# First feed-forward product in two sums: both parts of the input behind one load of the high weights

## The chip, the core and the metric

The kernel runs on one core of a Trainium2 chip. The metric is the device time of one execution in microseconds (us), the median of several runs. Weights and inputs lie in HBM as float32; the kernel loads them, computes on the core's engines (TensorE, VectorE, ScalarE, GpSimd, and SyncE for the transfers) and writes a result of 256 x 1024.

## The reference

A first block of other layers is followed by two layers like this one (`DEPTH_2` is 2, the width 1024, 256 tokens, the inner width 4096):

```python
for l in range(DEPTH_2):
    h = _rms_norm(x, attn_norm[l])
    ...
    x = x + mixed @ w_out[l]
    h = _rms_norm(x, mlp_norm[l])
    x = x + jnp.square(jax.nn.relu(h @ w_ff1[l])) @ w_ff2[l]
return _rms_norm(x, final_norm)
```

The change touches `h @ w_ff1[l]` and what stands right around it: the relu and the square behind it, and the start of `... @ w_ff2[l]`.

## The kernel before

**Split numbers.** Products of the layers are made of float32 values in two parts of the type float32r: `high`, the rounded value, and `low`, the rest. A product is then high x high, plus high weights x low input, plus low weights x high input. The input of the first feed-forward product lies in `xh` and `xl`, each 128 partitions x (8 chunks of 256 tokens), viewed as `xhT` and `xlT`.

**Units.** Weights come in units of 512 KB (128 x 1024), through a ring of four slots (class `Ring`). For each unit ScalarE makes the high part (`Ring.round`, L184, the rounding) and GpSimd the low part (`Ring.subtract`, L199). Both parts have two buffers, so the rounding of unit n waits until TensorE is done with all of unit n - 2, and the subtraction of unit n for its rounding. Every engine runs its instructions in the order of its own program; waits are on semaphores.

**The stage.** The first feed-forward product has 32 units, 128 of the 4096 inner columns each. Two units make a pair i (0 to 15), one PSUM bank of 512 float32: unit 2i fills its columns 0 to 255, unit 2i + 1 the rest. `split_pair` (L1998 on) issues 24 matmuls per unit, all at L2008: 8 with high weights and `xhT`, 8 with high weights and `xlT`, 8 with low weights and `xhT`, 256 columns each.

What follows for each pair i:
- `relu(i)` on VectorE (L1966), in the bank, over 512 columns
- `hidden(i)` on ScalarE: Square in the bank (L1701), then a Copy into `hidden_hi` (L1703)
- `hidden_low(i)` on VectorE (L1972): bank minus `hidden_hi` into `hidden_lo`; with it the bank is released

VectorE issues `relu(i)` and then `hidden_low(i - 1)`. ScalarE's loop (i from 1 to 15) issues a rounding, then `hidden(i - 1)` (pairs 0 and 1 at i = 3, pairs 2 and 3 at i = 4), then a second rounding. The first waits for the end of unit 2i, the second for the end of unit 2i + 1.

**Banks.** Class `Banks` hands the eight banks of PSUM to named jobs by a plan made ahead (L1490 to L1496). `open` on TensorE waits until all earlier jobs of that bank were given back (`give`); `take` on another engine waits until the bank is full. Before, pairs 0 and 1 hold banks 4 and 5, pairs 2 to 5 the banks 0 to 3, and pairs 6 to 15 the banks 4 to 6 in turn. Bank 7 holds constants.

**The second product** follows: 32 units of 24 matmuls (L2306), which sum into banks 0 to 3. All four are opened ahead of its first matmul:

```python
out_banks = [banks.open(pe, ("f2", l, b)) for b in range(4)]
for u in range(FF2_UNITS):
    high = ring.high(pe)
    banks.wait_drained(pe, ("f", l, u // 2))
```

Other places that the text refers to: the down rows of the mixture stage ahead of the layers (`down_row`, L2627 and L2634), 12 matmuls of 512 columns per row of weights, of the same types; the square roots and row sums of the layers (L1994, L1559); the attention's transposes (L422 to L424) and the output product of the attention (`branch`, L2064, L2069).

Of the kernel before, what the change touches and what calls it, by code (L numbers as in the profile page):

```python
# [20 lines left out]
F32R = mybir.dt.float32r  # L21
# [249 lines left out]
def build(nc, stop_after, xT, consts, par1, bias1, w1, keys, wu, wv, par2, w2, out):  # L271
    ctx = ExitStack()
    with ctx:
        def sb(name, cols, dt=F32):
            return ctx.enter_context(nc.sbuf_tensor(name, [P, cols], dt))

        def sem(name):
            return ctx.enter_context(nc.semaphore(name))
# [7 lines left out]

        xh, xl = sb("xh", DC * T, F32R), sb("xl", DC * T, F32R)
        wh, wl = sb("wh", 2 * SLOT, F32R), sb("wl", 2 * SLOT, F32R)
# [5 lines left out]
        arena = memory.enter_context(nc.sbuf_tensor("arena", [P, ARENA], F32))  # L294
        xhT, xlT = (x[:, :].rearrange("p (c t) -> p c t", t=T) for x in (xh, xl))
        whv, wlv = (x[:, :].rearrange("p (b n) -> p b n", b=2) for x in (wh, wl))
# [31 lines left out]
        def two(ap, w=T):  # L328
            return ap.rearrange("p (a b) -> p a b", b=w)
# [62 lines left out]
        def pairs_of(names):  # L392

            return [x for n in names for x in (None, n)]
# [993 lines left out]
        def lview(at, a, b):  # L1388
            return lpart(at, at + a * b).rearrange("p (a b) -> p a b", b=b)
# [53 lines left out]
        MLA, SELECTED, WINDOW = 2, 0, 1  # L1443
        l_pre, l_tiles = sem("squares_added"), sem("tile_sum_matrix")
        tile_sum = small[:, 1792:1824]
        nsa_heads = [[2 * c, 2 * c + 1, 8 + 2 * c, 9 + 2 * c] for c in range(4)]
# [9 lines left out]
        for l in range(LAYERS):  # L1456
# [34 lines left out]
            banks.turn = 0  # L1491
            banks.plan([("f", l, i) for i in range(2, 6)], low4)
            banks.turn = 0
            banks.plan([("f", l, i) for i in range(6, 16)], mid3)
            for b in low4:
# [6 lines left out]
            ring.plan(banks, [("wn", l, i) for i in range(4)] + [("wm", l, i) for i in range(4)]  # L1502
                      + pairs_of([("f", l, i) for i in range(16)]) + [None] * 31 + [("f2", l, 3)], True)
        banks.plan([("end", 0)], (4,))
# [34 lines left out]
        def layers_act(act):  # L1539
# [34 lines left out]
            for l in range(LAYERS):  # L1574
# [122 lines left out]
                def hidden(i):  # L1697
# [5 lines left out]
                    act.activation(hidden_hi[:, 2 * i:2 * i + 2, :], two(b[:, :]), ACT.Copy).then_inc(l_fhi, 1)  # L1703

                for i in range(1, 16):
                    ring.round(act, 1)
                    if i == 3:
                        hidden(0)
                        hidden(1)
                    elif i == 4:  # L1710
                        hidden(2)
                        hidden(3)
                    elif i > 4:
                        hidden(i - 1)
                    ring.round(act, 1)
                hidden(15)
                ring.round(act, FF2_UNITS - 2)
# [7 lines left out]
        def layers_dve(dve):  # L1725
# [29 lines left out]
            for l in range(LAYERS):  # L1755
# [212 lines left out]
                def hidden_low(i):  # L1968
# [4 lines left out]
                                                 ALU.subtract), ("f", l, i))  # L1973

                for i in range(17):
                    if i < 16:
                        relu(i)
                    if i:
                        hidden_low(i - 1)
# [7 lines left out]
        def layers_pe(pe):  # L1987
# [91 lines left out]
            for l in range(LAYERS):  # L2079
# [212 lines left out]
                for i in range(4):  # L2292
                    branch(("wm", l, i), l, 4, i == 0)
                    if i == 0:
                        sums(("mm", l), (1,), added, ready=(l_pre, 6 * l + 4))
                for i in range(16):
                    split_pair(("f", l, i), 2 * l + 1 if i == 0 else None)
                    if i == 1:
                        sums(("mf", l), range(2), added, ready=(l_pre, 6 * l + 6))
# [564 lines left out]
```

## Time and profile before

| | |
|---|---|
| median of 3 runs | 1742.39 us (1741.98 to 1742.43) |
| the profiled execution | 1742.68 us, of which 1740.9 us from the first to the last instruction (the span) |
| mean granted TensorE clock | 0.990 |
| TensorE (PE) busy | 1651.7 us, 95% |
| VectorE (DVE) busy | 895.1 us, 51% |
| ScalarE (ACT) busy | 917.8 us, 53% |
| GpSimd (POOL) busy | 1193.6 us, 69% |
| HBM read | 277.3 MB, 160 GB/s over the span |

Times in the trace are in us from the start of the span. PE is TensorE's matmuls and PEld its weight loads, which run beside them. A matmul's duration in a row is longer than the distance to the next, since matmuls are pipelined; distances are read from start to start. In brackets stands how long the engine had been idle and what released it. The first feed-forward product runs from about 1201 to 1299 us in the first layer and from about 1539 to 1637 us in the second.

### The profile page before, as it was taken

Reading aid. Unit: us, or ns where it says so; the run is one execution under the profiler, and the core shown is the slowest. Engines: PE = TensorE matmul, PEld = TensorE weight load, DVE = VectorE, ACT = ScalarE, POOL = GpSimd, SP = SyncE. Lnnn points to the kernel's source line nnn. Section 1 sums busy time; section 2 is a strip of 40 time slices with the busy share of each in tenths; the row PEclk is TensorE's granted clock in tenths of the full one; section 3 lists DMA queues with packets and bytes.
Section 4 is the critical chain, followed back from the end, with each engine's and each line's share of the span. In section 5 each row is a group of like instructions: output and inputs, shape, how many; then the busy total and the mean of one; then the engine's idle time right before and its main releaser. Section 6 shows DMA issues by size and latency. Waiting matters only on the chain.

```text
span 1740.9 us, 32150 instructions
## 1 busy us (share of the span) xinstructions
PE 1651.7 (95%) x12786; PEld 1506.7 (87%) x12786; DVE 895.1 (51%) x1888; ACT 917.8 (53%) x1541; POOL 1193.6 (69%) x500
## 2 busy tenths in 40 slices
PE   6988999999999999999999999888999998989997
PEld 6976999999999998777788888667999986789997
DVE  6978446991266665788611115866220067652101
ACT  5576655444543435555566665565553446655532
POOL 4552777888777777777788887115888861168885
PEclk9999999999999999999999999999999999999999
DMA  6432555655555555555566664513656654145663
GB/s 209 159 103 68 184 166 172 182 183 181 174 166 167 163 169 165 164 169 166 182 193 193 193 194 144 178 46 116 179 184 183 187 153 157 50 133 183 185 190 110
DMA packets 79604, 280.43 MB, mean 161 GB/s; under 512 B 8672, under 2 KB 9440, under 8 KB 79200
## 3 DMA queue, kind: packets, MB, share of 16 engines
q1 hardware_dynamic: 79456, 278.38, 51.8%
q8 instruction: 102, 1.67, 0.4%
q14 instruction: 46, 0.38, 0.1%
HBM read 277.30 MB, written 1.05 MB: 160 GB/s over the span
## 4 chain that ended last, share of the span: by engine, by line
PE 63%; issue 4%; DVE 3%; POOL 2%; ACT 1%; POOLq 0%; DVEq 0%; ACTq 0%
PE ps L2627 14%; PE ps L2008 12%; PE ps L2306 10%; PE ps L2634 7%; PE ps L2605 4%; PE ps L2606 3%; PE ps L2610 3%; POOL wl L199 2%; PE ps L2064 1%; PE ps L2591 1%; PE ps L371 1%; PE ps L2593 1%; PE ps L2130 1%; DVE small L390 1%; PE ps L2069 1%
## 5 line engine op out<-in xcount | busy, mean ns | idle before, releaser
L199 POOL TENSOR_TENSOR wl<-slots,wh 128x1024 fp32r<-128x1024 f32 x236 | 569.7, 2417 | 377.9 <-ACT wh L184 370.8
L2413 POOL TENSOR_TENSOR wl<-slots,wh 128x1024 fp32r<-128x1024 f32 x256 | 619.1, 2420 | 153.5 <-ACT wh L2353 151.4
L2353 ACT ACTIVATE wh<-slots 128x1024 fp32r<-128x1024 f32 x256 | 271.3, 1060 | 378.9 <-issue 244.9
L184 ACT ACTIVATE wh<-slots 128x1024 fp32r<-128x1024 f32 x236 | 249.4, 1060 | 263.5 <-PE ps L2306 105.5
L2605 PE MATMUL ps<-xh,wh 128*128 128x256 f32 x1024 | 255.6, 287 | 0.9 <-ACT small L2392 0.9
L2606 PE MATMUL ps<-xl,wh 128*128 128x256 f32 x1024 | 250.4, 282 | 0.0
L2605 PEld LDWEIGHTS ps<-xh,wh 128*128 128x128 f32 x1024 | 195.5, 191 | 1.2 <-ACT small L2392 1.1
L2606 PEld LDWEIGHTS ps<-xl,wh 128*128 128x128 f32 x1024 | 195.9, 191 | 0.0
L2627 PE MATMUL ps<-wh,xh 128*128 128x512 f32 x508 | 162.1, 400 | 2.8 <-DVE xl L2539 2.8
L2627 PE MATMUL ps<-wh,xl 128*128 128x512 f32 x508 | 157.7, 392 | 0.0
L2610 PE MATMUL ps<-xh,wl 128*128 128x256 f32 x1024 | 143.6, 283 | 0.6 <-POOL wl L2413 0.6
L2539 DVE TENSOR_TENSOR xl<-ps,xh 128x256 fp32r<-128x256 f32 x127 | 53.9, 424 | 161.8 <-ACT xh L2369 161.7
L2634 PE MATMUL ps<-wl,xh 128*128 128x512 f32 x508 | 136.3, 390 | 0.0
L2610 PEld LDWEIGHTS ps<-xh,wl 128*128 128x128 f32 x1024 | 132.1, 192 | 0.8 <-POOL wl L2413 0.8
L2306 PE MATMUL ps<-hidden_hi,wh 128*128 128x256 f32 x512 | 124.3, 280 | 1.9 <-POOL wl L199 1.9
L2306 PE MATMUL ps<-hidden_lo,wh 128*128 128x256 f32 x512 | 124.0, 279 | 0.0
L2634 PEld LDWEIGHTS ps<-wl,xh 128*128 128x128 f32 x508 | 95.4, 188 | 20.9
L2627 PEld LDWEIGHTS ps<-wh,xl 128*128 128x128 f32 x508 | 95.3, 188 | 20.6
L2008 PE MATMUL ps<-xh,wh 128*128 128x256 f32 x704 | 105.8, 289 | 6.9 <-ACT wh L184 4.6
L2627 PEld LDWEIGHTS ps<-wh,xh 128*128 128x128 f32 x508 | 91.0, 189 | 19.2 <-issue 3.2
L2008 PEld LDWEIGHTS ps<-xh,wh 128*128 128x128 f32 x704 | 92.4, 191 | 13.4 <-issue 8.0
L2531 DVE SCALAR_TENSOR_TENSOR arena<-ps,arena 128x256 f32<-128x256 f32 x128 | 54.0, 423 | 94.3 <-PE ps L2593 94.3
(383 smaller groups left out, 3140.5 us busy)
## 6 DMA issues: line engine op xcount, KB each, us to landing
slots<-w SPq DMA_DIRECT2D x260, 512.0 KB, 3.6
slots<-wu SPq DMA_DIRECT2D x128, 512.0 KB, 3.5
slots<-wv SPq DMA_DIRECT2D x128, 512.0 KB, 3.5
arena<-bias SPq DMA_DIRECT2D x1, 2048.0 KB, 8.1
h<-xT SPq DMA_DIRECT2D x2, 512.0 KB, 5.4
arena<-keys SPq DMA_DIRECT2D x1, 1024.0 KB, 5.7
yT<-y_out SPq DMA_DIRECT2D x2, 512.0 KB, 2.7
layer<-consts SPq DMA_DIRECT2D x1, 800.0 KB, 5.3
```

The source lines that it names most:

```text
L184: act.activation(self.hi[:, n % 2, :], self.slots[:, u % SLOTS, :], ACT.Copy).then_inc(self.rounded, 1)
L199: pool.tensor_tensor(self.lo[:, n % 2, :], self.slots[:, self.order[n] % SLOTS, :], self.hi[:, n % 2, :].bitcast(F32), ALU.subtract).then_ ...
L2008: ins = pe.matmul(halves[j], w[:, k, :], x[:, k, :], start=(first and k == 0), stop=(last and k == DC - 1), skip_group_check=True)
L2306: return pe.matmul(out_banks[c // 2][:, (c % 2) * T:(c % 2 + 1) * T], w[:, c * P:(c + 1) * P], x[:, u, :], start=start, stop=False, skip_g ...
L2353: act.activation(whv[:, r % 2, :], slots_v[:, r % SLOTS, :], ACT.Copy).then_inc(w_hi, 1)
L2413: pool.tensor_tensor(wlv[:, r % 2, :], slots_v[:, r % SLOTS, :], whv[:, r % 2, :].bitcast(F32), ALU.subtract).then_inc(w_lo, 1)
L2531: dve.scalar_tensor_tensor(a, grid, 1.0 / GATE_SCALE, a, ALU.mult, ALU.mult).then_inc(g_done, 1)
L2605: pe.matmul(out, hi[:, k, :], xhT[:, k, :], start=(k == 0), stop=False)
L2606: ins = pe.matmul(out, hi[:, k, :], xlT[:, k, :], start=False, stop=False)
L2610: ins = pe.matmul(out, lo[:, k, :], xhT[:, k, :], start=False, stop=(k == DC - 1))
L2627: ins = pe.matmul(psum[2 * t + half], part_a[:, tokens], hi[:, half * 512:(half + 1) * 512], start=begins, stop=False, skip_group_check=True)
L2634: ins = pe.matmul(psum[2 * t + half], a_hi[:, t * P:(t + 1) * P], lo[:, half * 512:(half + 1) * 512], start=False, stop=(row == NE2 - 1), ...
```

## The change

Pairs 2 to 15 are computed otherwise; pairs 0 and 1 stay. `xh` and `xl` become two halves of one tensor, so that one view, `x_parts[:, :, k, :]`, gives chunk k of both parts, 2 x 256 columns. A unit now has a bank of its own (jobs `f` and `f_second`). Eight matmuls of 512 columns with the high weights leave two sums in it, one per input part, and eight matmuls of 256 columns with the low weights add to the first. ScalarE copies the second sum into SBUF (`keep_second`), and VectorE adds it to the first (`add_halves`); for the pair's second unit the sum is written into the other half of the bank of `f`, after which `relu`, `hidden` and `hidden_low` go on as before, and the bank of `f_second` is given back. The 28 jobs of a layer take banks 0 to 6 in turn.

```diff
-        xh, xl = sb("xh", DC * T, F32R), sb("xl", DC * T, F32R)
+        both = sb("x_parts", 2 * DC * T, F32R)
+        xh, xl = both[:, 0:DC * T], both[:, DC * T:2 * DC * T]
+        x_parts = both[:, :].rearrange("p (k c t) -> p k c t", k=2, t=T)
...
+        l_half, l_both = sem("second_half_kept"), sem("halves_added")
+        second_half = lview(5888, 2, T)
...
             banks.turn = 0
-            banks.plan([("f", l, i) for i in range(2, 6)], low4)
-            banks.turn = 0
-            banks.plan([("f", l, i) for i in range(6, 16)], mid3)
+            banks.plan([(n, l, i) for i in range(2, 16) for n in ("f", "f_second")], seven)
             for b in low4:
                 banks.plan([("f2", l, b)], (b,))
...
-                      + pairs_of([("f", l, i) for i in range(16)]) + [None] * 31 + [("f2", l, 3)], True)
+                      + pairs_of([("f", l, i) for i in range(2)])
+                      + [(n, l, i) for i in range(2, 16) for n in ("f", "f_second")] + [None] * 31 + [("f2", l, 3)], True)
...
+                def keep_second(i, j):
+
+                    b = banks.take(act, (("f", "f_second")[j], l, i))
+                    if j == 0 and 14 * l + i > 2:
+                        act.wait_ge(l_both, 14 * l + i - 2)
+                    elif j == 1 and i > 2:
+                        banks.wait_drained(act, ("f_second", l, i - 1))
+                    act.activation(second_half[:, j, :], b[:, T:2 * T], ACT.Copy).then_inc(l_half, 1)
+
                 for i in range(1, 16):
                     ring.round(act, 1)
                     if i == 3:
                         hidden(0)
                         hidden(1)
                     elif i == 4:
                         hidden(2)
                         hidden(3)
                     elif i > 4:
                         hidden(i - 1)
+                    if i >= 2:
+                        keep_second(i, 0)
                     ring.round(act, 1)
+                    if i >= 2:
+                        keep_second(i, 1)
                 hidden(15)
...
+                def add_halves(i):
+
+                    b = banks.take(dve, ("f", l, i))
+                    dve.wait_ge(l_half, 28 * l + 2 * (i - 2) + 1)
+                    dve.tensor_tensor(b[:, 0:T], b[:, 0:T], second_half[:, 0, :], ALU.add).then_inc(l_both, 1)
+                    other = banks.take(dve, ("f_second", l, i))
+                    dve.wait_ge(l_half, 28 * l + 2 * (i - 2) + 2)
+                    banks.give(dve.tensor_tensor(b[:, T:2 * T], other[:, 0:T], second_half[:, 1, :], ALU.add),
+                               ("f_second", l, i))
+                    dve.wait_ge(l_both, 14 * l + i - 1)
+                    banks.wait_drained(dve, ("f_second", l, i))
+
                 for i in range(17):
+                    if 2 <= i < 16:
+                        add_halves(i)
                     if i < 16:
                         relu(i)
                     if i:
                         hidden_low(i - 1)
...
+                def wide_unit(job):
+
+                    bank = banks.open(pe, job)
+                    w = ring.high(pe).rearrange("p (k n) -> p k n", k=DC)
+                    for k in range(DC):
+                        pe.matmul(two(bank[:, :]), w[:, k, :], x_parts[:, :, k, :], start=(k == 0), stop=False,
+                                  skip_group_check=True)
+                    w = ring.low(pe).rearrange("p (k n) -> p k n", k=DC)
+                    for k in range(DC):
+                        ins = pe.matmul(bank[:, 0:T], w[:, k, :], xhT[:, k, :], start=False, stop=(k == DC - 1),
+                                        skip_group_check=True)
+                    banks.close(ins, job)
+
                 for i in range(16):
+                    if i >= 2:
+                        wide_unit(("f", l, i))
+                        wide_unit(("f_second", l, i))
+                        continue
                     split_pair(("f", l, i), 2 * l + 1 if i == 0 else None)
```

## Rows read from the trace of the kernel before

**Rows 1.** The page, busy time, share of the span and instructions of the engines.

```profile
PE 1651.7 (95%) x12786; PEld 1506.7 (87%) x12786; DVE 895.1 (51%) x1888; ACT 917.8 (53%) x1541; POOL 1193.6 (69%) x500
```

**Rows 2.** Busy time by window, main stretch of the stage in both layers.

```profile
core 0: us, PE busy (x) PEld busy (x) DVE busy (x) ACT busy (x) POOL busy (x), PEclk, DMA share, GB/s
1221.19:1298.95 77.76, 77.76 (x650) 77.76 (x649) 17.26 (x27) 44.69 (x57) 65.32 (x28) 1.00 0.61 185
1559.23:1637.00 77.77, 77.77 (x651) 77.77 (x650) 17.26 (x27) 44.68 (x57) 65.33 (x28) 1.00 0.59 185
```

**Rows 3.** Timeline of TensorE, one unit and the next one's start: start, length, instructions.

```profile
1247.12 1.12 PE L2008 MATMUL ps<-xh,wh 128*128 128x256 f32 x8
1248.08 1.12 PE L2008 MATMUL ps<-xl,wh 128*128 128x256 f32 x8
...
1249.99 1.12 PE L2008 MATMUL ps<-xh,wh 128*128 128x256 f32 x8
```

**Rows 4.** Busy time by window, down rows of the mixture stage (columns as in rows 2).

```profile
868.80:1010.25 141.45, 141.45 (x626) 117.13 (x625) 22.13 (x52) 87.01 (x157) 125.17 (x53) 1.00 0.63 193
```

**Rows 5.** The chain that ended last, near pair 2's first unit: start, length, what.

```profile
1217.69 2.40 POOL wl L199
1220.09 0.04 issue
```

**Rows 6.** Groups of instructions by shape, ScalarE, 256 columns from PSUM (mean ns second).

```profile
L1545 ACT ACTIVATE xh<-ps,layer_par 128x256 fp32r<-128x256 f32 x32 | 12.3, 482 | 4.6 <-DVE ps L1955 1.9 <-DVE ps L1731 1.5 <-DVE ps L1752 1.2
L1630 ACT ACTIVATE attention<-ps 128x256 f32<-128x256 f32 x16 | 6.1, 384 | 16.0 <-PE ps L2130 16.0
```

**Rows 7.** Groups of instructions by shape, VectorE, 256 columns with one input from PSUM.

```profile
L2508 DVE TENSOR_TENSOR ps<-ps,small 128x256 f32<-128x256 f32 x128 | 54.1, 423 | 0.1
L2539 DVE TENSOR_TENSOR xl<-ps,xh 128x256 fp32r<-128x256 f32 x127 | 53.9, 424 | 161.8 <-ACT xh L2369 161.7
```

**Rows 8.** Timeline of ScalarE in the stage, a rounding and pair 0's Square and Copy.

```profile
1227.21 1.06 ACT L184 ACTIVATE wh<-slots 128x1024 fp32r<-128x1024 f32 x1 [1.82 <-PE ps L2008]
1228.18 0.58 ACT L1701 ACTIVATE ps<-ps 128x512 f32<-128x512 f32 x1
1228.79 0.60 ACT L1703 ACTIVATE hidden_hi<-ps 128x512 fp32r<-128x512 f32 x1
1229.29 0.60 ACT L1701 ACTIVATE ps<-ps 128x512 f32<-128x512 f32 x1
```

**Rows 9.** Timeline of VectorE in the stage, `hidden_low(0)` and the relu behind it.

```profile
1229.49 0.69 DVE L1972 TENSOR_TENSOR hidden_lo<-ps,hidden_hi 128x512 fp32r<-128x512 f32 x1 [9.71 <-ACT hidden_hi L1703]
1230.10 0.69 DVE L1966 SCALAR_TENSOR_TENSOR ps<-ps,rst 128x512 f32<-128x512 f32 x1
```

**Rows 10.** Timeline of all engines where the second product starts, first layer.

```profile
1298.95 0.28 PE L2306 MATMUL ps<-hidden_hi,wh 128*128 128x256 f32 x1
...
1299.21 1.06 ACT L184 ACTIVATE wh<-slots 128x1024 fp32r<-128x1024 f32 x1 [0.70 <-PE ps L2008]
```

**Rows 11.** Timeline of TensorE around three gaps of the attention part.

```profile
1112.69 1.96 PE L2194 MATMUL ps<-attention,slots 128*128 128x256 f32 x8 [2.48 <-issue]
...
1139.21 0.45 PE L422 MATMUL ps<-cst,attention 128*128 128x128 f32 x1 [3.06 <-issue]
...
1169.23 0.71 PE L1994 MATMUL ps<-small,cst 128*128 128x256 f32 x2 [2.07 <-DVE small L390]
1169.55 2.10 PE L2064 MATMUL ps<-mix_hi,wh 128*128 128x256 f32 x8
1171.45 1.86 PE L2064 MATMUL ps<-mix_lo,wh 128*128 128x256 f32 x8
1173.16 1.10 PE L2069 MATMUL ps<-mix_hi,wl 128*128 128x256 f32 x8
1174.10 1.10 PE L2064 MATMUL ps<-mix_hi,wh 128*128 128x256 f32 x8
1175.03 1.10 PE L2064 MATMUL ps<-mix_lo,wh 128*128 128x256 f32 x8
```

**Rows 12.** Busy time and granted clock by window, behind or at the same gaps.

```profile
1140.00:1142.00 2.00, 2.00 (x11) 1.88 (x10) 1.90 (x7) 1.47 (x3) 2.00 (x2) 0.50 0.00 0
1170.00:1172.00 2.00, 2.00 (x11) 2.00 (x11) 0.46 (x1) 2.00 (x8) 1.64 (x1) 0.50 0.04 8
1111.00:1114.00 3.00, 1.31 (x6) 1.21 (x7) 1.49 (x2) 1.64 (x7) 0.00 (x0) 1.00 1.02 412
```

More of the change, by code:

```diff
@@ L294, in build @@
         arena = memory.enter_context(nc.sbuf_tensor("arena", [P, ARENA], F32))
-        xhT, xlT = (x[:, :].rearrange("p (c t) -> p c t", t=T) for x in (xh, xl))
+        xhT, xlT = (x.rearrange("p (c t) -> p c t", t=T) for x in (xh, xl))
         whv, wlv = (x[:, :].rearrange("p (b n) -> p b n", b=2) for x in (wh, wl))
```

## The prediction

> **What bounds the kernel now.** I read the page's share of busy time first: TensorE is busy for 95% of the span, every other engine for 69% or less [rows 1]. Then the same numbers by stretch, because the change touches one stage only, the first feed-forward product of the two layers. In both layers its main stretch is 77.76 us long and TensorE is busy for all of it, at full granted clock, with GpSimd at 65 us and ScalarE at 45 us [rows 2]. So TensorE sets the time of the stage, and a shorter unit of TensorE work is worth its full length as long as nothing else becomes late. The stretch holds 27 of the stage's 32 units, 2.880 us each; a group of eight 256-column matmuls takes 0.96 us, that is 120 ns a matmul, 24 to a unit [rows 3].
>
> **What the change removes.** In a changed unit the 16 matmuls with high weights become 8 of 512 columns. The trace has 512-column matmuls of the same types, in the down rows of the mixture stage: 52 rows of 12 in 141.45 us, so 226.7 ns each [rows 4]. A unit becomes 8 x 226.7 + 8 x 120 = 2.773 us, 0.107 us less. Pairs 2 to 15 change, 28 units in a layer. The first of them gains nothing: its low weights wait for GpSimd, whose subtraction ends at 1220.09, and TensorE goes on at 1220.13 [rows 5]; the subtraction's start doesn't depend on the high part. Gain: 27 x 0.107 = 2.88 us a layer, 5.8 us in all. The one difference from the down rows is that the 512 moving columns lie in two pieces of 256, 8 KB apart in a partition. No row shows such a read. The bounds for the wide matmul are 213 ns (512 columns at 2.4 GHz) and 240 ns (no gain over two of 256); I take 226.7, since the engine reads column by column either way.
>
> By the Trainium skill, "TensorE: Matmul & The Clock Gate", section "Back-to-back issue gap", a matmul costs its columns at 2.4 GHz plus 2.5 ns, so that joining two saves only 2.5 ns. Rows 3 and 4 disagree: 256 columns cost 13.3 ns over their 106.7, and 512 cost 13.4 ns over their 213.3.
>
> **What it adds, with cover.** ScalarE gets two copies of 256 columns per pair, the rows nearest being 384 and 482 ns [rows 6]; I take 0.42. VectorE gets two additions of 256 columns, 424 ns each [rows 7], and waits for its own result. With pairs of 5.55 us, ScalarE holds two roundings (0.97 each, start to start), Square and Copy (1.11) and the copies (0.8): 3.9 us [rows 8]. VectorE holds 0.9 + 0.6 + 0.7 = 2.2 us [rows 9]. Both fit. Does order fit? After a unit ends, ScalarE starts the next rounding 0.26 us later [rows 10], GpSimd subtracts for 2.4 us [rows 5], and the result is there about 3.8 us after the unit's end; TensorE asks for it 2.77 + 1.81 = 4.6 us after. The work in front of the second rounding (rounding, Square, Copy, copy: 0.26 + 0.97 + 1.11 + 0.42 = 2.76) ends just as that rounding becomes due at 2.77 + 0.26. The steady state is hidden at no cost; if cover were missing by x, it would cost x on each of 28 pairs once the slack of 0.8 us is used.
>
> **Banks.** The plan now gives seven banks in turn to (f, f_second) of pairs 2 to 15. That moves two waits.
> (a) f of pair 4 gets bank 4, which pair 0 held. Pair 0 is released by `hidden_low(0)`, which waits for ScalarE's Square and Copy, and those stand behind the rounding that waits for f of pair 3. Before, that bank was asked for much later, by pair 6. With units of 2.773 from 1221.19 on, where the window of rows 2 begins, f of pair 3 is the second unit and ends at 1226.74. Rounding starts 0.26 later, the Copy 1.58 after that (0.97 + 0.61) and takes 0.60; 0.10 to VectorE, 0.69 for the subtraction, 0.04 to TensorE: 1230.0 [rows 5, 8, 9, 10]. TensorE wants the bank after the third unit, at 1229.51. Cost 0.5 us a layer. Just behind it ScalarE has two hidden pairs and two copies to do, its rounding comes 0.8 us late, and TensorE waits some 0.1 us more; 0 to 0.6 are the bounds.
> (b) Counting on, pair 14's f is job 24 of the turn, so bank 3; pairs 12 and 13 hold banks 0 to 2 last. The second product opens banks 0 to 3 before its first matmul. Before, pairs 2 to 5 held these banks last, and the second product started with no gap at 1298.95 [rows 10]. Now TensorE waits for `hidden_low(14)`. In VectorE's program that stands behind `add_halves(15)` and `relu(15)`, and `add_halves(15)` needs the very last unit and ScalarE's copy of it, which itself stands behind a rounding that waits for the same unit. From the end of the last unit (time 0): rounding starts 0.26 [rows 10]; the copy at 1.23 [rows 8]; done 1.65; VectorE 0.10 later adds for 0.42, until 2.17; 0.04 for its own wait (taken as TensorE's); `relu(15)` starts at 2.21 and `hidden_low(14)` 0.61 behind it, at 2.82; plus 0.68 is 3.50; plus 0.04 [rows 5 to 9]. TensorE stands for 3.5 us, once a layer. Bounds: 3.3 (copy at 384 ns, no wait between) and 3.8. Nothing gives it back: the second product is TensorE's alone, with GpSimd at 2.4 us of each 2.8 us unit, and rounding for its third unit can't start before its first ends.
>
> **Clock.** Such a gap has a second price. In the attention part TensorE stood for 3.06 us and for 2.07 us, and behind each the granted clock is 0.50, that is 1.2 GHz of 2.4; after a gap of 2.48 us it stayed at 1.00 [rows 11, 12]. The same holds in the other layer, where the gaps repeat. Behind the 2.07 us gap two groups of eight take 1.90 and 1.71 us from start to start where such a group takes 0.93: 1.75 us lost [rows 11]. The new gap of 3.5 us is longer than all of these, so I expect the fall. Bounds 0 and 1.75; I take 1.6, because part of the slow stretch may lie in the gap itself.
>
> **Sum.** Per layer: -2.88 + 0.5 + 0.1 + 3.5 + 1.6 = +2.8 us. Two layers: +5.6. The profiled execution took 1742.68 us (span 1740.9), 0.3 above the median of 1742.39, so the forecast for the median is 1748.0 us.
>
> **The rivals.**
> 1. The hand-over stall is there, but the clock stays up, in one layer or both. For: the 2.48 us gap left it alone. Against: two of three kinds of gap did not, and this one is longer. Without any fall, 2 x 1.2 = +2.4: 1744.8 us. With one, 1746.4.
> 2. Joining saves nothing, because the fixed cost is not per matmul or the two pieces read slower. Then the 5.8 us stay: 1753.8 us. Against: rows 3 and 4 give the same 13 ns for both widths. The skill's rule named above goes most of the way there; by it alone the saving would be 54 x 8 x 2.5 ns = 1.1 us, an estimate from that page, and the time 1752.7.
> 3. ScalarE's longer queue makes the second rounding late in each pair, not only near pair 4. For: its margin before that rounding is only 0.3 us. Against: 0.8 us of slack behind it at TensorE. It decides from about 1.1 us of lateness; at 0.3 us a pair it costs 28 x 0.3 = 8 us: 1756 us. Also against: the copies' nearest rows leave no room for 1.1 us.
> 4. The other side: bank 3 does not bind at the hand-over, as when pair 14 is released ahead of the last unit (a slip in my count of the turn, or in the order of VectorE's program). The stall and the clock's fall go together: -2 x 2.88 + 2 x 0.6 = -4.6, so 1737.8 us. It decides from a stall below 2.3 us a layer without a fall. For: only the release of one bank separates the cases. Against: job 24 of seven is 3, and the code issues `hidden_low(i - 1)` behind `add_halves(i)` and `relu(i)`.
> 5. The bank or copy waits are shorter than I price them, by up to 1 us a layer, and the clock falls in one layer: 2 x (-2.88 + 0.6 + 2.5) + 1.6 = +2.0, 1744.4 us.
>
> **Numbers.** Forecast 0.52; rival 1 0.18, half within 0.2%; rival 2 0.08; rival 3 0.06; rival 4 0.08; rival 5 0.08. A change of 0.2%, 3.5 us, is about what a measurement of this kernel can tell from none: 1738.9 to 1745.9 is "same". Faster 0.08, same 0.09 + 0.08 = 0.17, slower 0.75. The range runs from 1744.3 (rival 5; rival 1 without a fall is just above) to 1754.5 (rival 2, with the bounds of a and b on the forecast); it leaves out rivals 3 and 4.
>
> **What would show it.** In the profile after: a changed unit of 2.77 us, wide matmuls 227 ns apart; a gap on TensorE of about 0.5 us ahead of pair 4; a gap of 3.5 us ahead of each first matmul of the second product, ended by VectorE's `hidden_lo`; a granted clock of 0.50 behind it for some 3 us; the stage itself about 2.2 us shorter a layer, and the second product late by what I say. A wide matmul 240 ns apart, a hand-over without a gap, or a TensorE wait for GpSimd in each pair would prove me wrong, each at its own step.

## The result, and the profile after

The median of five runs is 1751.88 us (1749.43 to 1752.61), beside 1742.43 us for five runs of the kernel before (1741.98 to 1745.21). The ratio is 1.0047, with a 95% interval of 1.0033 to 1.0062: the change makes the kernel slower by 9.5 us where 5.6 were forecast. The profiled execution took 1751.99 us, its span is 1750.2.

The page of after, the answer to rows 1. TensorE has 448 matmuls fewer and is busy for longer:

```profile
PE 1654.2 (95%) x12338; PEld 1489.0 (85%) x12338; DVE 918.7 (52%) x1944; ACT 933.6 (53%) x1597; POOL 1193.2 (68%) x500
```

**Where the time is.** I set the same points of TensorE's program side by side, each by the start of the matmul there.

| point | before | after | behind by | gained since |
|---|---|---|---|---|
| first layer begins | 1051.29 | 1051.30 | 0.0 | |
| pair 2 begins | 1217.75 | 1218.57 | 0.8 | +0.8 |
| second product begins | 1298.95 | 1301.89 | 2.9 | +2.1 |
| second layer begins | 1390.59 | 1395.58 | 5.0 | +2.1 |
| its pair 2 begins | 1555.79 | 1560.35 | 4.6 | -0.4 |
| its second product begins | 1636.99 | 1643.66 | 6.7 | +2.1 |
| last matmul of it | 1728.49 | 1737.81 | 9.3 | +2.6 |

So both products of both layers lose. The 0.8 us ahead of the first pair 2 is outside the change: the granted clock falls once more there, in the attention part. It falls behind the very gap of 2.4 us that left the clock alone in the trace of before [rows 11, 12] (window of after, columns as in rows 2):

```profile
1113.60:1116.60 3.00, 3.00 (x18) 2.26 (x18) 1.65 (x4) 2.98 (x12) 0.00 (x0) 0.50 0.63 258
```

The -0.4 us between the start of the second layer and its pair 2 lies outside the change as well.

The main stretch of the stage in after, to be read against rows 2 (busy time by window, same columns). It is 76.02 us where it was 77.76, and a gap now follows it that the stretch doesn't include:

```profile
1222.01:1298.03 76.02, 75.69 (x434) 66.31 (x432) 28.39 (x53) 52.19 (x84) 64.97 (x28) 1.00 0.59 189
```

The timeline of TensorE in after, against rows 3: a wide group, a low group, and so on. Eight wide matmuls take 1.84 us from start to start and the low ones 0.95, a unit 2.79 us (2.88 before). The third row to the last shows the wait ahead of pair 4:

```profile
1224.81 2.00 PE L2332 MATMUL ps<-x_parts,wh 128*128 128x512 f32 x8
1226.65 1.12 PE L2336 MATMUL ps<-x_parts,wl 128*128 128x256 f32 x8
1227.60 2.00 PE L2332 MATMUL ps<-x_parts,wh 128*128 128x512 f32 x8
1229.44 1.11 PE L2336 MATMUL ps<-x_parts,wl 128*128 128x256 f32 x8
1230.89 2.11 PE L2332 MATMUL ps<-x_parts,wh 128*128 128x512 f32 x8 [0.34 <-DVE hidden_lo L1988]
1232.84 1.11 PE L2336 MATMUL ps<-x_parts,wl 128*128 128x256 f32 x8
1233.79 2.00 PE L2332 MATMUL ps<-x_parts,wh 128*128 128x512 f32 x8
```

The hand-over, as the chain that ended last has it in after (start, length, what). It is the answer to rows 10, where the second product followed without a gap. Read down: the last low group, ScalarE's rounding, its copy of the second sum, VectorE's second addition, `relu(15)`, `hidden_low(14)`, and then the second product. The trace calls `second_half` by the name of the tensor that it lies in, `attention`:

```profile
1297.24 0.96 PE ps L2336 x8
...
1298.28 0.04 ACT wh L184
...
1299.25 0.37 ACT attention L1715
...
1299.71 0.44 DVE ps L1998
...
1300.24 0.06 DVE ps L1982
1300.30 0.55 issue
1300.84 0.69 DVE hidden_lo L1988
1301.54 0.35 issue
1301.89 1.20 PE ps L2354 x4
```

The last 0.35 us, between the end of `hidden_low(14)` and the first matmul, hold three wait instructions of TensorE's own program, about 0.11 us from one to the next. The first is the wait for bank 3 itself, in `open` (L106). Behind it stand that of `ring.high` (L213) and that for pair 0 in the second product's loop (L126), whose work had long been done. `PEldq` is the sequencer of TensorE's weight loads. Each has one row (shortest, median and longest duration in ns, first and last start):

```profile
L106 PEldq EVENT_SEMAPHORE  x1: 51/51/51, 1301.6 to 1301.6; - x1
L213 PEldq EVENT_SEMAPHORE  x1: 51/51/51, 1301.7 to 1301.7; - x1
L126 PEldq EVENT_SEMAPHORE  x1: 51/51/51, 1301.8 to 1301.8; - x1
```

Behind the hand-over the second product starts slowly. The timeline of TensorE in after: matmuls stand 0.21 us apart where they stand 0.12 before and later.

```profile
1301.89 0.55 PE L2354 MATMUL ps<-hidden_hi,wh 128*128 128x256 f32 x1 [3.70 <-DVE hidden_lo L1988]
1302.24 0.42 PE L2354 MATMUL ps<-hidden_lo,wh 128*128 128x256 f32 x1
...
1305.44 1.91 PE L2354 MATMUL ps<-hidden_hi,wl 128*128 128x256 f32 x8
1307.15 0.41 PE L2354 MATMUL ps<-hidden_hi,wh 128*128 128x256 f32 x1
...
1309.43 1.10 PE L2354 MATMUL ps<-hidden_hi,wl 128*128 128x256 f32 x8
```

Busy time and granted clock by window for it, both layers (columns as in rows 2):

```profile
1302.00:1308.00 6.00, 6.00 (x28) 6.00 (x29) 0.69 (x1) 0.73 (x2) 0.00 (x0) 0.50 0.28 88
1644.00:1649.00 5.00, 5.00 (x25) 5.00 (x25) 0.69 (x1) 0.00 (x0) 0.00 (x0) 0.50 0.35 108
```

**The first layer's account.** The stretch: -1.74 us. From the end of the last unit, 1298.03, to the second product, 1301.89: +3.86. The first two units of the second product take 5.26 and 3.21 us where they took 2.83 each: +2.81, the clock. The rest of the second product, from its third unit to the next layer, takes 85.22 us where it took 85.98: -0.76. With the +0.8 from ahead of the stage this is the 5.0 of the table. In the second layer the first two units take 5.26 and 3.04 us, +2.64, and the rest takes as long as before: its units are 2.83 us there, and 2.80 in the first layer. So the 0.76 us came in one layer only.

### The profile page after: what moved, and what is told of

Read it like the earlier page. It is cut to its first block, busy times and chain, and to the rows that moved or that the text cites. A ratio compares the mean times of both kernels' runs of the same rounds, so it can differ in the third digit from the quotient of the medians.

```text
span 1750.2 us, 31531 instructions
## 1 busy us (share of the span) xinstructions
PE 1654.2 (95%) x12338; PEld 1489.0 (85%) x12338; DVE 918.7 (52%) x1944; ACT 933.6 (53%) x1597; POOL 1193.2 (68%) x500
## 4 chain that ended last, share of the span: by engine, by line
PE 64%; issue 3%; DVE 3%; POOL 2%; ACT 1%; POOLq 0%; DVEq 0%; ACTq 0%
PE ps L2675 14%; PE ps L2354 10%; PE ps L2682 7%; PE ps L2332 5%; PE ps L2653 4%; PE ps L2654 3%; PE ps L2658 3%; PE ps L2038 3%; PE ps L2336 3%; POOL wl L199 1%; PE ps L2094 1%; PE ps L2639 1%; PE ps L2106 1%; PE ps L373 1%; PE ps L2641 1%
## 5 line engine op out<-in xcount | busy, mean ns | idle before, releaser
L2675 PE MATMUL ps<-wh,x_parts 128*128 128x512 f32 x1016 | 258.2, 396 | 2.8 <-DVE x_parts L2587 2.8
L2653 PE MATMUL ps<-x_parts,wh 128*128 128x256 f32 x1024 | 255.5, 287 | 0.9 <-ACT small L2440 0.9
L2654 PE MATMUL ps<-x_parts,wh 128*128 128x256 f32 x1024 | 250.4, 282 | 0.0
L2675 PEld LDWEIGHTS ps<-wh,x_parts 128*128 128x128 f32 x1016 | 186.3, 188 | 39.8 <-issue 3.2
L2653 PEld LDWEIGHTS ps<-x_parts,wh 128*128 128x128 f32 x1024 | 195.5, 191 | 1.2 <-ACT small L2440 1.1
L2654 PEld LDWEIGHTS ps<-x_parts,wh 128*128 128x128 f32 x1024 | 195.9, 191 | 0.0
L2658 PE MATMUL ps<-x_parts,wl 128*128 128x256 f32 x1024 | 143.6, 283 | 0.6 <-POOL wl L2461 0.6
L2682 PE MATMUL ps<-wl,x_parts 128*128 128x512 f32 x508 | 136.3, 390 | 0.0
L2658 PEld LDWEIGHTS ps<-x_parts,wl 128*128 128x128 f32 x1024 | 132.1, 192 | 0.8 <-POOL wl L2461 0.8
L538 PE MATMUL ps<-x_parts,wh 128*128 128x256 f32 x736 | 105.2, 298 | 22.7 <-ACT wh L184 9.4
L538 PEld LDWEIGHTS ps<-x_parts,wh 128*128 128x128 f32 x736 | 98.3, 203 | 27.3 <-ACT wh L184 15.8
L2332 PE MATMUL ps<-x_parts,wh 128*128 128x512 f32 x448 | 112.5, 393 | 3.9 <-ACT wh L184 3.2
L2682 PEld LDWEIGHTS ps<-wl,x_parts 128*128 128x128 f32 x508 | 95.4, 188 | 21.0
L2354 PEld LDWEIGHTS ps<-hidden_hi,wh 128*128 128x128 f32 x512 | 98.8, 193 | 10.0 <-issue 10.0
```

The lines of the kernel that those rows point to most:

```text
L538: ins = pe.matmul(halves[j], w[:, k, :], x[:, k, :], start=(first and k == 0), stop=(last and k == DC - 1), skip_group_check=True)
L2332: pe.matmul(two(bank[:, :]), w[:, k, :], x_parts[:, :, k, :], start=(k == 0), stop=False, skip_group_check=True)
L2354: return pe.matmul(out_banks[c // 2][:, (c % 2) * T:(c % 2 + 1) * T], w[:, c * P:(c + 1) * P], x[:, u, :], start=start, stop=False, skip_g ...
L2653: pe.matmul(out, hi[:, k, :], xhT[:, k, :], start=(k == 0), stop=False)
L2654: ins = pe.matmul(out, hi[:, k, :], xlT[:, k, :], start=False, stop=False)
L2658: ins = pe.matmul(out, lo[:, k, :], xhT[:, k, :], start=False, stop=(k == DC - 1))
```

## The experiments

Theory: the wide matmuls gain what their spacing says, and a late release of bank 3 makes the gap, behind which the clock falls. Rivals: the loss sits in something that the additions or copies do in each pair; the slow start isn't the clock's; the gap would be given back. Ratios are to runs of the kernel before that were made beside those of the experiments: 21 runs for `e1_banks` to `e4_best` (1741.7 to 1746.3 us) and 31 for `e5_adjacent` to `e8_order` (1740.9 to 1748.1). A difference of two ratios carries both intervals, some 3 us either way. Each trace shows one execution.

**Only the last four banks** (`e1_banks`). The kernel after with

```diff
-            banks.plan([(n, l, i) for i in range(2, 16) for n in ("f", "f_second")], seven)
+            banks.plan([(n, l, i) for i in range(2, 14) for n in ("f", "f_second")], seven)
+            for n, i, b in (("f", 14, 4), ("f_second", 14, 5), ("f", 15, 6), ("f_second", 15, 5)):
+                banks.plan([(n, l, i)], (b,))
```

> The kernel after, with one edit: the last four jobs (f and f_second of pairs 14 and 15) take banks 4, 5, 6, 5 and not 3, 4, 5, 6, so no bank that the second product opens is held by pair 14 or 15. Theory (the late release of bank 3 makes a 3.9 us gap at TensorE and behind it the clock falls, 2.8 us more, per layer): both go, 2 x 6.7 = 13 us less than after, about 1738.5 us; no TensorE gap ahead of the second product, granted clock 1.00 there. Rival (the time is lost elsewhere: the second product only inherits work that is late anyway, ScalarE's and VectorE's rest of pair 15 or GpSimd's next subtraction): a gap appears at another wait just behind, and the time stays within 4 us of after, 1748 or more.

Measured: 1740.72 us median, ratio 0.9987 (0.9977 to 0.9997). Against after that is 0.6%, some 10.4 us by the ratios, give or take 3. TensorE's timeline shows the second product right behind the last low group, and the window behind it has the full clock:

```profile
1296.06 1.11 PE L2338 MATMUL ps<-x_parts,wl 128*128 128x256 f32 x8
1297.01 0.28 PE L2356 MATMUL ps<-hidden_hi,wh 128*128 128x256 f32 x1
```

```profile
1297.00:1303.00 6.00, 6.00 (x53) 6.00 (x52) 2.85 (x5) 3.53 (x6) 4.21 (x3) 1.00 0.60 202
```

Other banks for four jobs turn the kernel from slower to faster. The rival is out. The gain is below the 13 us expected, though the interval reaches that far. A reason for less can be seen further below: the clock does not fall behind each hand-over gap of after, so its mean price is under 2.8 us a layer.

**The same cause from VectorE's side** (`e8_order`). The kernel after with its own bank plan, and

```diff
                 for i in range(17):
+                    if i == 15:
+                        hidden_low(14)
                     if 2 <= i < 16:
                         add_halves(i)
                     if i < 16:
                         relu(i)
-                    if i:
+                    if i and i != 15:
                         hidden_low(i - 1)
```

> The kernel after with its own bank plan; only VectorE's program is changed: hidden_low(14) stands ahead of add_halves(15) and relu(15), not behind them. Theory (bank 3 is late because hidden_low(14) queues behind work of pair 15): ScalarE's Copy for it ends 0.35 us ahead of the last unit's end, so the gap shrinks from 3.9 to about 0.5 us and the clock stays up: about 1739.5 us, ratio 0.998. Rival (the bank is late for another reason, such as ScalarE's part): the gap stays near 3.7 us and the time at 1752.

Measured: 1741.88 us, ratio 0.9989 (0.9979 to 0.9999). The gap is 0.65 us in both layers and the clock stays up (first layer):

```profile
1298.94 0.36 PE L2356 MATMUL ps<-hidden_hi,wh 128*128 128x256 f32 x1 [0.65 <-DVE hidden_lo L1988]
```

So what stood ahead of `hidden_low(14)` in VectorE's program made 3.05 of the 3.70 us. Of the 0.65 us that are left, 0.35 are again the three waits of TensorE's program (the chain behind `hidden_low(14)`):

```profile
1298.59 0.35 issue
1298.94 0.36 PE ps L2356
```

**Filling the gap** (`e2_fill`). The kernel after with a job more in the bank plan and, ahead of the second product, 30 matmuls:

```diff
+            banks.plan([("fill", l)], (4,))
...
+                bank = banks.open(pe, ("fill", l))
+                for n in range(30):
+                    ins = pe.matmul(bank[:, 0:T], xhT[:, 0, 0:P], xhT[:, n % DC, :], start=(n == 0), stop=(n == 29),
+                                    skip_group_check=True)
+                    if n == 28:
+                        banks.close(ins, ("fill", l))
+                banks.give(ins, ("fill", l))
                 out_banks = [banks.open(pe, ("f2", l, b)) for b in range(4)]
```

> The kernel after with 30 extra matmuls of 256 columns between the two products of each layer, into bank 4 once pair 14 has released it; nothing reads them. They last 3.6 us and fill the gap. Theory (gap and clock are two prices, 3.9 and 2.8 us a layer): the second product starts no earlier than in after, but the granted clock stays at 1.00, so 2 x 2.8 = 5.6 us less than after: about 1746 us. Rival (the slower matmuls behind the gap are not the clock's but come of the restart or of something that the second product shares with ScalarE and VectorE then): no gain, 1751 to 1753.

Measured: 1746.02 us, ratio 1.0014 (1.0004 to 1.0024), 5.7 us less than after by the ratios, give or take 3. The second product starts just as late, 3.87 us behind the last unit, but at full clock (timeline, then the window behind it):

```profile
1298.72 3.76 PE L2351 MATMUL ps<-x_parts 128*128 128x256 f32 x30
...
1302.59 0.36 PE L2362 MATMUL ps<-hidden_hi,wh 128*128 128x256 f32 x1
```

```profile
1303.00:1308.00 5.00, 5.00 (x45) 5.00 (x44) 0.68 (x1) 1.06 (x1) 1.13 (x1) 1.00 0.31 108
```

Gap and clock are two prices. Useless matmuls in the gap save 5.7 us, beside the 5.4 (2.8 and 2.6) that the clock took in the trace of after. That the two numbers lie so close is partly luck: in other executions of after the clock falls less often (see `e9_again`).

**The stall alone** (`e3_wait`). The kernel before with one line ahead of the second product:

```diff
+                banks.wait_drained(pe, ("f", l, 15))
                 out_banks = [banks.open(pe, ("f2", l, b)) for b in range(4)]
```

> The kernel before with one wait added: ahead of the second product TensorE waits for hidden_low(15). No wide matmul, no additions, old banks. In the trace of before hidden_low(15) ends 3.2 us after the second product's start, so the wait makes a gap of 3.3 us a layer. Theory: the gap alone costs 3.3 and the clock behind it 1.7 to 2.8 a layer, 10 to 12 us in all: 1752.5 to 1754.6. Rival (part of such a gap is given back later in the layer, at waits that then find their work done): clearly less than 6.6 us, under 1748.

Measured: 1752.15 us, ratio 1.0051 (1.0034 to 1.0068), 8.9 us. A kernel with no wide matmul and no addition becomes as slow as after by a wait at this place. Its gap is 3.12 us in both layers (first layer, then the windows behind both):

```profile
1305.24 0.38 PE L2307 MATMUL ps<-hidden_hi,wh 128*128 128x256 f32 x1 [3.12 <-DVE hidden_lo L1972]
```

```profile
1306.00:1309.00 3.00, 3.00 (x16) 3.00 (x15) 0.00 (x0) 0.00 (x0) 0.00 (x0) 0.51 0.59 178
1647.00:1650.00 3.00, 3.00 (x17) 3.00 (x17) 0.00 (x0) 0.00 (x0) 0.27 (x1) 0.56 0.63 209
```

It lies a little under the 10 to 12 expected, which the interval (5.9 to 11.9 us) covers. Its second product then runs in units of 2.80 us where before has 2.83. That isn't the gap given back: the best version below has 2.80 without any gap, and the second layer of after has 2.83 behind one.

This kernel also tells what the last 0.35 us of after's gap are. Here the added wait ends last, no wait instruction stands between it and the first weight load, and the second product starts 0.05 us behind `hidden_low(15)`, after a stop of 3.12 us (the chain):

```profile
1304.49 0.70 DVE hidden_lo L1972
1305.19 0.04 issue
1305.24 0.38 PE ps L2307
```

So the 0.35 us do not come of a long stop. They stand where the wait for bank 3 ends last, an instruction of its own with two more behind it: in after behind 3.70 us, in `e8_order` behind 0.65.

**A shorter gap** (`e7_gap2`). As the first experiment, but f_second of pair 15 takes bank 0 and not 5.

> The kernel e1_banks, but f_second of pair 15 takes bank 0, which add_halves(15) releases 2.2 us after the last unit, ahead of relu(15) and hidden_low(14). It gives a hand-over gap of some 2.1 us in place of 3.7. Theory (the gap decides both prices): 2.1 us plus a fall of the clock for 3.4 us (1.7 us) in each layer, as behind the 2.07 us gap of rows 11: 2 x 3.8 = 7.6 us more than e1_banks, ratio to before about 1.003. If a gap of 2.1 us leaves the clock alone there: 4.2 us more, ratio 1.001. Rival (gap and clock are proportional to nothing that the bank decides): same as e1_banks or same as after.

Measured: 1744.76 us, ratio 1.0010 (1.0001 to 1.0019). The same gap of 2.02 us stands in both layers, and only in the first does the clock fall behind it:

```profile
1301.11 0.58 PE L2356 MATMUL ps<-hidden_hi,wh 128*128 128x256 f32 x1 [2.02 <-DVE ps L2000]
...
1639.82 0.38 PE L2356 MATMUL ps<-hidden_hi,wh 128*128 128x256 f32 x1 [2.02 <-DVE ps L2000]
```

```profile
1301.00:1304.00 3.00, 2.89 (x13) 2.89 (x14) 2.04 (x4) 1.18 (x2) 1.70 (x1) 0.52 0.59 186
1640.00:1643.00 3.00, 3.00 (x27) 3.00 (x28) 1.83 (x3) 1.20 (x3) 1.41 (x1) 1.00 0.61 183
```

Against the first experiment that is 0.23%, 4 us, give or take 2 to 3: the two gaps alone are 4.0. In the trace, half of the falls that I forecast did not come; what the clock costs on average is too small here to tell from the times.

**After, once more** (`e9_again`).

> The kernel after, unchanged, for a second trace of it. In the first one both layers show the granted clock at 0.50 for 6.8 us behind the hand-over gap of 3.7 us, twice the 3.4 us of each gap in rows 11 and 12. Theory A (that length belongs to this gap, which is longer): again 6.8 us in both layers, and 2.8 us lost in each. Theory B (it hangs on where the gap falls in time, as in e7_gap2, where the same gap of 2.0 us brought a fall in one layer and none in the other): 3.4 us in one layer or in both, and a time up to 3 us shorter.

Measured, a single run: 1750.85 us. The gap is 3.70 us in both layers again. Behind the first the clock is low for 6.8 us, behind the second not at all (windows, TensorE idle for the start of each):

```profile
1303.00:1308.00 5.00, 3.49 (x16) 3.52 (x17) 1.84 (x3) 1.18 (x2) 1.39 (x1) 0.50 0.55 197
1644.00:1649.00 5.00, 3.12 (x27) 3.15 (x28) 2.12 (x4) 1.18 (x2) 1.75 (x1) 1.00 0.60 208
```

So theory A is out: even a gap of 3.7 us doesn't bring the fall every time. Theory B has the variation right and the length wrong, since the one fall is again 6.8 us long and not 3.4; that it hangs on where the gap falls in time is not shown. What one is worth can be read here without a model: from the start of the second layer's second product to its second low group it is 4.75 us in this run and 7.36 in the first trace, 2.6 us apart.

**The width alone, and the best version** (`e4_best` and `e6_split`). Two kernels. The first is the first experiment's, with ScalarE's work on pairs 0 and 1 a turn earlier, which takes the wait ahead of pair 4 away:

```diff
-                    if i == 3:
+                    if i == 2:
                         hidden(0)
                         hidden(1)
-                    elif i == 4:
-                        hidden(2)
-                        hidden(3)
-                    elif i > 4:
+                    elif i > 2:
                         hidden(i - 1)
```

> The kernel e1_banks, and ScalarE's Square and Copy of pairs 0 and 1 stand one turn earlier (i = 2, then one pair each turn), so that bank 4 is free when pair 4 opens it. Theory: the last stall of 0.5 us a layer goes too; what is left of the change is 27 units of 0.09 us a layer, 4.8 us: about 1737.5 us, 1 us under e1_banks. Rival (the work moved forward makes the second rounding of pair 2 or 3 late, or the additions cost TensorE something in each pair): no better than e1_banks, or a new wait for GpSimd in pairs 2 to 4.

Measured: 1738.22 us (1737.42 to 1739.81), ratio 0.9970 (0.9958 to 0.9983). TensorE waits for VectorE nowhere in either product. This is 5.2 us better than before, and 13.4 us better than after by the ratios.

The second undoes only the width in it:

```diff
-                        pe.matmul(two(bank[:, :]), w[:, k, :], x_parts[:, :, k, :], start=(k == 0), stop=False,
-                                  skip_group_check=True)
+                        for j, x in enumerate((xhT, xlT)):
+                            pe.matmul(bank[:, j * T:(j + 1) * T], w[:, k, :], x[:, k, :], start=(k + j == 0), stop=False,
+                                      skip_group_check=True)
```

> The kernel e4_best with each wide matmul made as two of 256 columns again, into the two halves of the same bank: banks, copies, additions and order stay, only the width of 512 is undone. Theory (the whole gain is the fixed time per matmul, seen as 0.09 us a unit): units of 2.88 us, 54 x 0.09 = 4.8 us slower than e4_best, about the time of before (ratio 1.000), since copies and additions are hidden. Rival (the additions and copies cost TensorE something in each pair, or the gain comes of the other bank plan): units other than 2.88 us, or a time clearly over before.

Measured: 1744.00 us, ratio 1.0002 (0.9992 to 1.0011). Its timeline has units of 2.88 us, as rows 3:

```profile
1241.93 2.08 PE L2332 MATMUL ps<-x_parts,wh 128*128 128x256 f32 x16
1243.85 1.12 PE L2336 MATMUL ps<-x_parts,wl 128*128 128x256 f32 x8
1244.81 2.08 PE L2332 MATMUL ps<-x_parts,wh 128*128 128x256 f32 x16
```

With the copies, the additions and the new banks but not the width, the time is that of the kernel before within 1.9 us: what ScalarE and VectorE were given is free in the first product. The width is worth 0.32%, 5.6 us, give or take 3, and the 4.8 from the spacing lie within that. The two traces differ in one thing more: the second product's units are 2.80 us in both layers of `e4_best` and 2.83 in both of `e6_split`, 0.8 us a layer. One trace of each can't say whether that belongs to the width.

**Why 230 ns and not 227** (`e5_adjacent` and `e10_allwide`). The best version with the two parts side by side for each chunk:

```diff
-        xh, xl = both[:, 0:DC * T], both[:, DC * T:2 * DC * T]
-        x_parts = both[:, :].rearrange("p (k c t) -> p k c t", k=2, t=T)
+        x_parts = both[:, :].rearrange("p (c k t) -> p k c t", k=2, t=T)
...
-        xhT, xlT = (x.rearrange("p (c t) -> p c t", t=T) for x in (xh, xl))
+        xhT, xlT = x_parts[:, 0], x_parts[:, 1]
```

> The kernel e4_best with the two parts of the input interleaved by chunk in x_parts, so that the 512 moving columns of a wide matmul lie side by side and not in two pieces 8 KB apart. In after and in e4_best eight wide matmuls take 1.84 us (230 ns each) where the down rows of before give 226.7. Theory A (the two pieces cost the 3.3 ns): eight take 1.81 us, a unit 2.77 us, 54 x 8 x 3.3 ns = 1.4 us less than e4_best, ratio to before about 0.9962. Theory B (the 3.3 ns come of what else runs at that time, or of the change of width): still 1.84 us a group, and the same time as e4_best.

Measured: 1737.27 us, ratio 0.9968 (0.9956 to 0.9979), the same as without. The groups still take 1.84 us. Reading two pieces 8 KB apart costs nothing that can be seen.

```profile
1241.27 2.00 PE L2330 MATMUL ps<-x_parts,wh 128*128 128x512 f32 x8
1243.11 1.11 PE L2334 MATMUL ps<-x_parts,wl 128*128 128x256 f32 x8
```

Then `e4_best` again, with the low weights made 512 columns wide as well:

```diff
-                        ins = pe.matmul(bank[:, 0:T], w[:, k, :], xhT[:, k, :], start=False, stop=(k == DC - 1),
+                        ins = pe.matmul(two(bank[:, :]), w[:, k, :], x_parts[:, :, k, :], start=False, stop=(k == DC - 1),
```

> The kernel e4_best with the low weights' matmuls of pairs 2 to 15 made 512 columns wide too, over both parts of the input, so that a term is added that the reference's sum in parts leaves out (low weights x low input) and no change of width is left inside the stage. In after, e4_best and e5_adjacent the first five wide matmuls of a unit stand 228 to 236 ns apart, the last three 227. Theory A (a wide matmul behind 256-column ones is slower for a while): all 16 of a unit 227 ns, a unit 3.63 us. Theory B (what ScalarE does in the first microsecond of a unit, its rounding, slows them): the first five stay at 228 to 236 ns, a unit 3.65 us. In either case about 54 x 0.85 = 46 us more than e4_best, some 1784 us.

Measured, a single run: 1785.70 us. Every group of eight, high or low, takes 1.81 or 1.82 us, so 227 ns a matmul, while ScalarE rounds as it did:

```profile
1262.75 1.98 PE L2331 MATMUL ps<-x_parts,wh 128*128 128x512 f32 x8
1264.57 1.98 PE L2335 MATMUL ps<-x_parts,wl 128*128 128x512 f32 x8
1266.38 1.98 PE L2331 MATMUL ps<-x_parts,wh 128*128 128x512 f32 x8
```

Theory A, from one trace: the extra time belongs to the change of width from 256 to 512 columns.

## Why the prediction came out as it did

The measured time lies inside the stated range and the kernel moved the way that was forecast, by the mechanism that was forecast. The sum was 3.9 us too low, and these are its terms.

**The gain** was sized too high. The step "a unit becomes 8 x 226.7 + 8 x 120" took the spacing from a stage in which all matmuls have one width [rows 4]. A unit measures 2.793 us, not 2.773; the gain is 27 x 0.087 = 2.35 us a layer and not 2.88. The first unit gained nothing, as said. The bounds of 213 and 240 ns held, and the doubt about the two pieces was about the wrong thing.

**Copies and additions** are hidden, as costed: 371 and 431 ns in after, and the width undone gives the time of before. Rival 3 is out, in the trace of after too, where TensorE never waits for GpSimd inside the steady pairs.

**The wait ahead of pair 4** was forecast as 0.5 us. The unit before it should have ended at 1230.39 and pair 4 began at 1230.89: 0.5. The further wait of 0.1 us behind it did not show, but the wide group behind the stop takes 1.95 us where the others take 1.84 (1230.89 to 1232.84 above), so 0.1 us was lost there by another way.

**The hand-over** was the step that decided, and its mechanism and place were right: bank 3, `hidden_low(14)`, the order on VectorE, with the copy behind the rounding. 3.5 us were forecast and 3.86 measured. The links on ScalarE and VectorE are right to 0.05 us each. What failed is the last one: I took 0.04 us from VectorE's end to TensorE's start, from a place where no other wait instruction stood between the wait that ended and the weight load. Here the wait for bank 3 is an instruction of its own, with two more behind it, and the way to the first matmul takes 0.35. It isn't the length of the stop: `e3_wait` starts 0.05 us behind VectorE after 3.12 us, and `e8_order` takes 0.35 after 0.65.

**The clock** was the term most wrong. I took 1.6 us, from falls of 3.4 us; here it stayed low for 6.8 us in both layers, 2.8 and 2.6 us. Filling the gap gives 5.7 us back, give or take 3. The premise was weak too: that a gap of 2.48 us left the clock alone was one outcome of a draw, since the trace of after has a fall behind the same gap. The part of the forecast that treated the fall as sure behind a long gap is right for these two and wrong as a rule, as the second trace of after shows. Rival 1 was thus not a rival but the other outcome of the same draw.

**What I left out.** 0.76 us came back in the second product of the first layer, against "nothing gives it back"; in the second layer none did, and other kernels show the same two speeds with and without a gap. And falls of the clock in the attention part move from run to run; the trace of after has one there that the trace of before hasn't, 0.8 us. Per layer the sum was 2.8 us, and the trace says 4.2 for the first and 4.7 for the second layer. That the range held the time owes something to its width: its upper end of 1754.5 came from rival 2, which is out.

Rival 2 (no gain from joining) and rival 4 (bank 3 does not bind) are out, by the width undone and by the new bank plan. The Trainium skill's rule, "TensorE: Matmul & The Clock Gate", section "Back-to-back issue gap", which the section gives for a matmul by itself, would give the width 1.1 us, an estimate from that page. The measurement differs: the two kernels that differ in the width alone lie 5.6 us apart, give or take 3.

## What to carry to other kernels

A change that hands out the buffers of a stage by another plan also changes who holds which of them when the stage ends. Follow the last few holders into the next stage, and read the program of the engine that frees them: here the late release of one bank outweighed the whole gain. Count the waits of the waiting engine's own program that stand behind the one that ends last. Where TensorE must stand for a few microseconds, price the slower clock behind it as well as the gap, from both outcomes; work without use in the gap can be cheaper than silence.

## What the runs showed of the hardware

- A wide matmul behind matmuls of 256 columns is slower for a while. In a unit of after the starts of the eight wide ones stand 234, 236, 228, 232, 231, 227, 227 and 226 ns apart, and the pattern repeats in each unit. With 512 columns throughout (`e10_allwide`, one trace) nearly all are 225 to 228. The eight take 26 ns more and the low group 8 ns less, so it costs about 18 ns a unit. What in the engine does it stays open.
- The granted clock behind a gap is a draw. A gap of 2.02 us brought a fall in one layer and none in the other; one of 3.70 us brought 6.8 us of half clock three times in four, and none once; 3.12 us brought 3.4 us in both layers. The three gaps of the attention part (rows 11) stand in both layers of all twelve traces. Half clock within 4.5 us behind them is the count: behind the one of 2.3 to 2.5 us 8 of 24, behind the one of 3.06 us 21, and behind the one of 2.04 to 2.08 us 18. So one trace doesn't tell whether a gap costs a fall.
- Wait instructions of TensorE follow each other some 0.11 us apart even where their work is done. With the wait that ended last in an instruction of its own and two more behind it, the first matmul came 0.35 us later, behind stops of 3.70 and 0.65 us alike. With no such instruction between, it came 0.05 us later, behind stops of 3.12, 2.02 and 0.34 us.
- The second product's units are 2.83 or 2.80 us long, with the same instructions at full clock, 117.8 or 116.7 ns a matmul, and from its fourth unit on a layer keeps one of the two, 0.8 us apart in all. Both layers of before have 2.83; after has 2.80 in the first layer and 2.83 in the second. In the first experiment the first layer's units are 2.83 and the second layer's go to 2.80 after its third unit. I have no cause for it.
